# A hybrid encoder layer on one core: convolution centring spread over four attention rows, and the routing table moved by one weight piece

## The reference

```python
def rmsnorm(x, g):
    return x * lax.rsqrt(jnp.mean(x * x, axis=-1, keepdims=True) + EPS) * g

def mixer(xn):                        # 512 x 1024
    glu_a, glu_g, q, k, v = split(xn @ w_in + b_in)      # five parts of 512
    u = depthwise_conv31(glu_a * sigmoid(glu_g)) + conv_b
    un = (u - mean(u)) * rsqrt(mean((u - mean(u))**2) + EPS) * ln_g + ln_b
    conv_out = silu(un)
    na_out = neighbourhood_attention(q, k, v, rpb)       # 8 heads of 64, windows of 8 x 16
    return concat(conv_out, na_out) @ w_out + b_out

def moe(xt):                          # top 4 of 32 experts, blocks of 128 tokens
    top_vals, top_idx = lax.top_k(xt @ w_router + b_router, 4)
    gates = softmax(top_vals)
    ...                               # each block of one expert e:
    gt = minimum(xb @ w_gate[e] + b_gate[e], 7); up = clip(xb @ w_up[e] + b_up[e], -7, 7)
    y = ((up + 1) * gt * sigmoid(1.702 * gt)) @ w_down[e] + b_down[e]
    ...                               # times its gate, summed per token

h = x + mixer(rmsnorm(x, g_mix));  h = h + moe(rmsnorm(h, g_ffn));  out = rmsnorm(h, g_final)
```

## Time and profile before

| what | us |
|---|---|
| median of 3 runs | 1460.7 (1459.77 to 1467.1) |
| the profiled execution, its own time | 1461.13 |
| its span, first to last instruction | 1459.0 |
| PE busy in the span | 1392.9 (95%) |
| DVE busy | 1270.6 (87%) |
| ACT busy | 966.9 (66%) |

### The profile page before, as it was taken

The page is one execution under the profiler, slowest core; times in us unless marked ns, Lnnn a source line. Parts: engine busy times, 40 slices in busy tenths (PEclk is TensorE's granted clock), DMA queues, the critical chain, the costliest instruction groups (busy, mean ns, idle before and its releaser), DMA issues.

```text
span 1459.0 us, 18730 instructions
## 1 busy us (share of the span) xinstructions
PE 1392.9 (95%) x6456; PEld 1150.2 (79%) x6456; DVE 1270.6 (87%) x996; ACT 966.9 (66%) x740; POOL 191.4 (13%) x191
## 2 busy tenths in 40 slices
PE   5999889689999999999999999999999999999995
PEld 4887667668888888888888888888888888888874
DVE  6899846789888888888888888888888888888898
ACT  3232644457777777777777777777777777777761
POOL 2000000011111111111111111111111111111063
PEclk9999779799999999999999999999999999999997
DMA  9922301799999999999999999999999999999983
GB/s 293 335 63 79 119 0 62 300 327 359 384 391 380 390 383 380 385 393 384 383 388 381 388 388 385 377 392 384 378 386 385 385 385 382 387 385 392 382 323 102
DMA packets 84977, 479.54 MB, mean 329 GB/s; under 512 B 10731, under 2 KB 11030, under 8 KB 35798
## 3 DMA queue, kind: packets, MB, share of 16 engines
q1 hardware_dynamic: 71982, 433.40, 76.4%
q0 software_dynamic: 6944, 25.18, 4.9%
q10 hardware_dynamic: 6024, 20.60, 3.6%
HBM read 449.82 MB, written 29.33 MB: 328 GB/s over the span
## 4 chain that ended last, share of the span: by engine, by line
PE 85%; DVE 10%; issue 2%; DMA 1%; ACT 1%; SPq 0%; POOL 0%; POOLq 0%; DVEq 0%; ACTq 0%
PE pair L1742 23%; PE pair L1740 23%; PE pair L1741 23%; DVE area_m L1012 3%; PE pair L1753 2%; PE pair L1727 2%; PE pair L1720 2%; DVE w_low L1166 1%; PE pair L1525 1%; PE pair L1526 1%; PE pair L1527 1%; DVE h L1438 1%; DVE win_low L987 1%; DMA h<-in_x 1%; PE pair L1606 1%
## 5 line engine op out<-in xcount | busy, mean ns | idle before, releaser
L1166 DVE TENSOR_TENSOR w_low<-w_raw,w_high 128x2048 fp32r<-128x2048 f32 x380 | 864.0, 2288 | 108.9 <-ACT w_high L770 106.1
L770 ACT CAST w_high<-w_raw 128x2048 fp32r<-128x2048 f32 x380 | 727.9, 1916 | 282.9 <-PE pair L1742 278.9
L1740 PE MATMUL pair<-w_high,xT_high 128*128 128x512 f32 x1008 | 395.0, 392 | 0.0
L1742 PE MATMUL pair<-w_high,xT_low 128*128 128x512 f32 x1008 | 393.0, 390 | 0.0
L1741 PE MATMUL pair<-w_low,xT_high 128*128 128x512 f32 x1008 | 392.4, 389 | 0.0
L1742 PEld LDWEIGHTS pair<-w_high,xT_low 128*128 128x128 f32 x1008 | 189.2, 188 | 39.6
L1741 PEld LDWEIGHTS pair<-w_low,xT_high 128*128 128x128 f32 x1008 | 189.3, 188 | 38.5
L1740 PEld LDWEIGHTS pair<-w_high,xT_high 128*128 128x128 f32 x1008 | 189.3, 188 | 38.4
L1740 PE MATMUL pair<-w_high,hT_high 128*128 128x512 f32 x496 | 195.8, 395 | 0.0
L1742 PE MATMUL pair<-w_high,hT_low 128*128 128x512 f32 x496 | 193.3, 390 | 0.0
L1741 PE MATMUL pair<-w_low,hT_high 128*128 128x512 f32 x496 | 193.2, 390 | 0.0
(11 more groups left out here) (300 smaller groups left out, 1411.0 us busy)
## 6 DMA issues: line engine op xcount, KB each, us to landing
w_raw<-in_w_gate SPq DMA_DIRECT2D x128, 1024.0 KB, 7.1
w_raw<-in_w_up SPq DMA_DIRECT2D x128, 1024.0 KB, 6.3
w_raw<-in_w_down SPq DMA_DIRECT2D x128, 1024.0 KB, 7.0
y_rows<-area_m ACTq DMA_DIRECT2D x30, 512.0 KB, 7.4
ring<-in_w_in SPq DMA_DIRECT2D x5, 2048.0 KB, 17.9
y_rows<-area_t SPq DMA_DIRECT2D x1, 8704.0 KB, 37.0
ring<-in_w_out SPq DMA_DIRECT2D x2, 2048.0 KB, 8.1
h<-in_x SPq DMA_DIRECT2D x4, 512.0 KB, 8.9
```

The source lines that it names most:

```text
L770: s.copy(w_high[:, i % HIGH_RING, :], w_raw[i][:, :]).then_inc(high_ready, 1)
L1166: v.tensor_tensor(w_low[i][:, :], w_raw[i][:, :], w_high[:, i % HIGH_RING, :].bitcast(F32), ALU.subtract).then_inc(low_ready, 1)
L1740: t.matmul(to[half], tok_high, hi, start=(opens and kk == 0), stop=False)
L1742: last = t.matmul(to[half], tok_low, hi, start=False, stop=(k == KD - 1))
```

## The change

- **Centring and squares.** DVE centres one channel group in each of rows 19 to 22, behind the scores of the row, and ACT squares one group in each of rows 20 to 23. The second block's `transpose_o` moves from row 18 to row 23 on PE, its high part from row 20 to 25 on ACT, its low part from row 21 to 26 on DVE. The four low parts of the output weight on DVE move from rows 20, 22, 24, 26 to rows 24, 26, 28, 30, the bias from row 24 to 23.
- **General table.** PE makes it after the second piece of block 0's gate part and not after the third. On DVE the low part of piece 4 moves ahead of the copy of the table.
- **Loads.** SP issues the loads of pieces 5 and 6 of block 0 behind the fetch of block 0's tokens, together with 7, 8, 9 and 11.
- **Bias.** In `gate`, the two matmuls of the bias come ahead of the wait for the low part of the tokens. For block 0 they get two waits of their own, for the routing step that last reads banks 0 and 1 and for the copy of the first table.

```diff
-        MEAN_AT, CENTRE_AT, SQUARE_AT, BOUT_AT = 16, 19, 20, 24
+        MEAN_AT, CENTRE_AT, SQUARE_AT, BOUT_AT, TURN_AT = 16, 19, 20, 23, 23
...
+        def turned_at(i, behind):
+            at = [10, TURN_AT, 26, 34]
+            return at.index(i - behind) if i - behind in at else None
...
-            for i in range(3, 7):
+            for i in range(3, 5):
                 load(i, 0)
...
-            for i in (7, 8, 9, 11):
+            for i in (5, 6, 7, 8, 9, 11):
                 load(i, 0)
...
-                if i == SQUARE_AT:
-                    for c in range(CC):
-                        act.wait_ge(centred, c + 1)
-                        s.activation(sq[:, c, :], mixedT[:, c, :], ACT.Square).then_inc(squared, 1)
+                if SQUARE_AT <= i < SQUARE_AT + CC:
+                    c = i - SQUARE_AT
+                    act.wait_ge(centred, c + 1)
+                    s.activation(sq[:, c, :], mixedT[:, c, :], ACT.Square).then_inc(squared, 1)
...
-            WOUT_AT = {20: 0, 22: 1, 24: 2, 26: 3}
+            WOUT_AT = {24: 0, 26: 1, 28: 2, 30: 3}
...
-                if i == CENTRE_AT:
+                if CENTRE_AT <= i < CENTRE_AT + CC:
+                    c = i - CENTRE_AT
                     dve.wait_ge(mean_done, 1)
                     dve.wait_ge(conv_tap, CONV_K * CC)
-                    for c in range(CC):
-                        v.tensor_tensor(mixedT[:, c, :], mixedT[:, c, :], bank[5][:, :], ALU.subtract).then_inc(centred, 1)
+                    v.tensor_tensor(mixedT[:, c, :], mixedT[:, c, :], bank[5][:, :], ALU.subtract).then_inc(centred, 1)
...
             low_part(3, 3)
+            low_part(4, 4)
             dve.wait_ge(table_done, 2)
...
             for i in range(DOWN):
                 at = i + AHEAD
-                if i:
+                if i >= 2:
                     low_part(at % DOWN, at)
...
             def gate(b, base, turn=None, high=xT_high, low=xT_low, between=None):
-                pe.wait_ge(xT_low_ready, b + 1)
                 pe.wait_ge(sel_in_ready, b + 1)
                 if not (isinstance(b, int) and b == 0):
                     pe.wait_ge(silu_done, b)
+                else:
+                    pe.wait_ge(route_step, NQ + 4)
+                    pe.wait_ge(table_ready, 1)
                 add_bias(G_TO, sel_gate, bias_gu)
+                pe.wait_ge(xT_low_ready, b + 1)
                 for i in range(4):
                     piece(GATE + i, base + i, high, low, G_TO)
                     if i == 1 and turn is not None:
                         transpose_h(turn)
-                    if i == 2 and between is not None:
+                    if i == 1 and between is not None:
                         between()
```

More of the change, by code:

```diff
@@ L736, in _ @@
                     s.activation(bout_rows[:, :], bout_raw, ACT.Copy, scale=16.0).then_inc(bout_high, 1)
-                n = normalised_at(i, 12)
+                n = turned_at(i, 2)
                 if n is not None:
                     attn_high_part(n)
-                if i == SQUARE_AT:
-                    for c in range(CC):
-                        act.wait_ge(centred, c + 1)
-                        s.activation(sq[:, c, :], mixedT[:, c, :], ACT.Square).then_inc(squared, 1)
+                if SQUARE_AT <= i < SQUARE_AT + CC:
+                    c = i - SQUARE_AT
+                    act.wait_ge(centred, c + 1)
+                    s.activation(sq[:, c, :], mixedT[:, c, :], ACT.Square).then_inc(squared, 1)
                 if i == NS:
@@ L1117, in _ @@
                     taps(2)
-                n = normalised_at(i, 13)
+                n = turned_at(i, 3)
                 if n is not None:
                     attn_low_part(n)
-                if i == CENTRE_AT:
+                if CENTRE_AT <= i < CENTRE_AT + CC:
+                    c = i - CENTRE_AT
                     dve.wait_ge(mean_done, 1)
                     dve.wait_ge(conv_tap, CONV_K * CC)
-                    for c in range(CC):
-                        v.tensor_tensor(mixedT[:, c, :], mixedT[:, c, :], bank[5][:, :], ALU.subtract).then_inc(centred, 1)
+                    v.tensor_tensor(mixedT[:, c, :], mixedT[:, c, :], bank[5][:, :], ALU.subtract).then_inc(centred, 1)
                 if i in WOUT_AT:
@@ L1636, in _ @@
                     pv(i - 1)
-                n = normalised_at(i, 10)
+                n = turned_at(i, 0)
                 if n is not None:
```

## The result

The changed kernel takes 1453.3 us, the median of 7 runs (1450.85 to 1456.27); the kernel before, measured beside it, 1461.24. The ratio over all executions of both is 0.9936, with a 95% interval of 0.9924 to 0.9948: 9.4 us faster (0.64%). The two medians alone are 7.9 us apart. The profiled execution took 1450.85 us, with a span of 1448.9, 10.1 shorter than the 1459.0 before. Executions of one kernel differ by some 5 us; what makes part of that is at the end.

What follows compares the result with a forecast made beforehand. PE bounds the expert loop and output projection, so gains come from the attention rows and the start of the experts: -5.0 - 4.6 - 0.4 = -10.0 from 1461.1, forecast 1451 us, range 1446.5 to 1458.5.

Steps and rivals of the forecast that it cites:

- the forecast's own case: Whole kernel: the summed gains arrive, 1451 us, own range 1447 to 1453; chance 0.58.
- The attention, -5.0: Attention rows 20 to 31: without ACT's lump, the sum of the squares starts at about 200.2 instead of 205.2, -5.0 us.
- the eight matmuls of the squares (5.28) I leave as they are: End of the attention rows, PE: the sum of the squares was taken to keep its 5.28 us.
- an idle of 1.89 us cost the clock: Attention, before row 21's transpose: PE's 1.89 us idle cost the clock, so 2 to 3 us around rows 26 and 27 would.
- The start of the experts, -4.6: Block 0's first pieces: DVE's 4.58 us idle before the general table's copy goes, hidden values end 4.58 us sooner.
- The table by 294.9, 0.9 us before DVE is free: Start of the experts: PE makes the general table by 294.9, so DVE's copy at 295.8 waits for nothing.
- The gather, -0.4 between 0 and -0.73: Fetch of block 0's tokens: two loads fewer ahead may shorten it, by 0 to 0.73 us, middle -0.4.
- The bias, 0: Block 0's gate: 1.19 us of PE's bias moves into its wait, giving nothing of its own.
- Rival 1: Attention, row 21: the clock is lost all the same, the order alone gives -2.3, 1453.8 us; chance 0.2.
- Rival 2: Attention: gives nothing, as DVE's work between rows 26 and 31 takes the gain; only -5.0, 1456.1 us; chance 0.08.
- Rival 3: Start of the experts: DVE waits 3.3 us for piece 5 instead of the table, 1454.4 us; chance 0.08.
- Rival 4: Loop over the experts: transfers pace it, ACT's casts wait for pieces, slower, 1469 us; chance 0.06.

Runs made afterwards that it cites:

- pieces 3 to 6 later: The changed kernel with the loads of pieces 3 and 4 also issued behind the fetch of block 0's tokens; ratio to the kernel before 0.9935.
- squares alone: The kernel before with one edit, ACT's squares one a row in rows 20 to 23 instead of four in row 20; ratio 0.9990.
- scores ahead of division: The changed kernel with DVE's low parts in rows 25 to 33 reordered and scores of rows 10, 18, 26 ahead of the division; 1446.39 us, 0.9898.
- attention alone: The kernel before with only the attention's edits (centring, squares, later turn of block 1, later low parts of the output weight); ratio 0.9972.
- start alone: The kernel before with only the other edits (general table, low part of piece 4, loads of pieces 5 and 6, bias); ratio 0.9973.
- table alone: The kernel before with only the general table made one piece of the gate sooner; ratio 0.9980.

## Why the prediction was right, and where it was off

The forecast was 1451 us, the median is 1453.3, the change is faster by over 0.5%. It came out as the forecast's own case; the median lies 0.3 us above that case's range (1447 to 1453) and inside the whole one (1446.5 to 1458.5).

**The attention, -5.0: right in kind, somewhat too large.** It is -4.68 in the profiled execution, -4.2 on the mean of five against four (-3.8 from the end of the mean), and -4.1 us by the time of that part alone. Row by row the count held to about 1 us, with all of it a little sooner: row 24's exponential 183.44 (183.9 forecast), block 2's division 185.85 (186.3), row 31's scores done at 196.40 (197.5), the sum of the squares 199.19 (200.2). That PE would idle some 2 to 3 us around rows 26 and 27 and lose its clock there was foreseen: it is 2.39 us, in pieces of 0.70, 0.25 and 1.44. The sentence that failed is "the eight matmuls of the squares (5.28) I leave as they are". They take 3.65 us at the full clock and up to 6.34 (pieces 3 to 6 later), and in the changed kernel they fall into the stretch at 1.2 GHz and take 6.17. That the sum came so near is partly luck: its matmuls start 0.8 us sooner against the kernel before than forecast and take 0.9 us longer. Also too simple was "an idle of 1.89 us cost the clock": squares alone has no idle time over 0.54 us and loses it, scores ahead of division has 0.71 and 0.87 and keeps it.

**The start of the experts, -4.6: right.** 4.57 us in the profiled execution, and between 36.7 and 37.0 us in all eight runs with these edits and block 0's hidden values at their old place. Its mechanism was DVE's 4.58 us ahead of the copy; each of the two edits fills half of it, as the two runs apart show. "The table by 294.9, 0.9 us before DVE is free" had little to spare: PE took pieces 0 and 1 in 7.1 us where 8.0 were counted, the table starts at 286.62 and lasts 1.86, so it is ready 1.7 us before the copy at 290.14; without the bias ahead, which was to give nothing of its own, it is 0.18 late.

**The gather, -0.4 between 0 and -0.73: -0.64.** The bias, 0: some 0.2. Both are too small for the time to tell.

**The rivals.** Rival 1 (the clock lost in row 21 all the same) did not happen: in 184 to 198 the clock is 0.86 in the changed kernel and 0.76 with the attention alone, for 0.51 before, and in all five runs it is 1.00 from 178 to 188. Rival 2 fell with the attention alone. Rival 3: DVE has no wait for piece 5. Rival 4: the waits of the loop are those of the earlier trace rows, ACT for PE and SP for free buffers, none for a transfer:

```profile
ACT w_high L774 <- PE pair L1747: 263.3, 362, 0.9
```

```profile
SPq L466 <- PE pair L1747: 842.0, 353, 3.2
SPq L501 <- PE pair L1747: 21.9, 4, 14.8
```

SP's first sum is 842.0 us for 851.4 before, but its other line has four waits, 21.9 us in all, where it had one of 14.8: with both it is 863.9 for 866.2, so its lead is as it was. The rule cited ahead of the result, to issue a transfer early (the Trainium skill, "DMA: Bandwidth & Descriptors", "Rules for kernel authors"), was rightly not followed here: with the two loads early the fetch interval is 0.64 us longer, and late they cost nothing.

**Why the median is 2 us above the forecast.** The sum of 10.0 was made against one profiled execution and came true in one (10.13 in the span), but that one, with 1450.85, is the fastest of the seven. The mean gains of the three intervals, 4.2 + 4.6 + 0.6 = 9.4, agree with the 9.4 us of the ratio, though its interval, 7.6 to 11.1, leaves room for other sums. So some 0.6 of the 2.3 us is the forecast's own error, most of it in the first term, which depends on where in rows 26 to 31 the clock falls; the rest is scatter of the executions, 5.4 us from the fastest to the slowest.

## What to carry to other kernels

Where PE is paced by short steps on two other engines, spread the extra work of both over the steps; taking the longest wait alone may give next to nothing, as here, where the clock fell with no wait over 0.54 us, and what runs next then pays for it at half speed. An engine's idle time ahead of one copy can be filled from two sides, work moved into it and its input made sooner, and its length is the most that the two can give. When a change's price hangs on the clock, take intervals from several executions before believing one.

## What was not expected of the hardware

The same idle time can cost the clock or not. Near the end PE waits for the last hidden values, 2.79 us in the changed kernel and 2.74 us in start alone, first the one, then the other:

```profile
1404.18 1.16 PE L1732 MATMUL pair<-ident,area_q 128*128 128x128 f32 x8 [2.79 <-DVE area_q L1344]
```

```profile
1410.14 1.38 PE L1728 MATMUL pair<-ident,area_q 128*128 128x128 f32 x8 [2.74 <-DVE area_q L1340]
```

Behind it the changed kernel has the clock at 1.00 and the other at 0.66 for 5 us:

```profile
1405.00:1410.00 5.00, 5.00 (x26) 4.15 (x25) 4.32 (x3) 4.62 (x3) 0.00 (x0) 1.00 1.02 409
```

```profile
1410.00:1415.00 5.00, 4.86 (x18) 4.08 (x19) 4.11 (x4) 2.81 (x2) 0.89 (x1) 0.66 1.01 411
```

From the hidden values of block 0 to the end of the span it is 1133.8 us in the one (1448.9 - 315.1) and 1135.5 in the other (1456.6 - 321.1). All fourteen profiled executions have this wait, of 2.73 to 2.79 us. In seven the clock is 1.00 in the 5 us behind it, and 44.7 or 44.8 us are left from its end to the end of the span: before, changed, attention alone, squares alone, table alone, pieces 3 to 6 later, scores ahead of division. In the other seven the clock is 0.66 to 0.71, and 46.1 to 46.5 us are left. So some 1.6 us of the difference between executions is the clock behind this one wait, and no edit explains on which side a run falls.

The Trainium skill, "TensorE: Matmul & The Clock Gate", section "Part 1: The HAM clock gate (the "warmup" mystery)", says that the stretch over which the clock gate watches the engine isn't started anew by a kernel, and that the point at which the clock rises therefore differs from run to run. It speaks of the rise at a kernel's start; these two rows are of a fall near a kernel's end, and fit it without showing that cause.
